# A two-layer decoder trunk: a longer table of small weights, and the first keys normed and rotated before the fifth weight split

## What is computed

```python
def reference(x, ...):
    # layer 0
    x = x + nsa_fox_mixer(rmsnorm(x, a_norm), a_w_in, ...)   # compressed, selected and window attention (8 heads, 2 key groups) + forgetting attention (8 heads)
    x = x + swiglu(rmsnorm(x, f_norm), f_w_gate, f_w_up, f_w_down)      # D_FF = 2816
    # layer 1
    x = x + gla_mixer(rmsnorm(x, c_norm), c_w_in, ...)                  # gated linear attention, 4 heads
    x = x + moe_ffn(rmsnorm(x, m_norm), m_router, m_w_gate, ...)        # best 2 of 8 SwiGLU experts
    return x

# in nsa_fox_mixer: the keys that this change touches
    ksl = partial_rope(rmsnorm(heads(ksl, G), nsa_k_norm), cos, sin)    # selected keys, 2 heads of 64
    kwn = partial_rope(rmsnorm(heads(kwn, G), nsa_k_norm), cos, sin)    # window keys, 2 heads of 64
```

## Time and profile before

| | |
|---|---|
| three runs | 1252.96 us median (1251.99 to 1253.08) |
| the profiled execution | 1252.75 us |
| its span, first to last instruction | 1250.9 us, so 1.85 us lie around it |
| busy: PE, DVE, ACT | 99%, 79%, 65% of the span |
| granted TensorE clock | 0.996 of full, mean |
| HBM read | 354.56 MB, mean 288 GB/s with the writes |

### The profile page before, as it was taken

One profiled execution on the slowest core, in us unless ns is written; L12 is line 12 of the kernel. 1 busy time (PEld: TensorE's weight loads), 2 busy tenths in 40 slices (PEclk: granted clock), 3 DMA queues, 4 the chain that ended last, 5 costly groups with the idle time before them and its releaser, 6 DMA issues.

```text
span 1250.9 us, 16182 instructions
## 1 busy us (share of the span) xinstructions
PE 1233.9 (99%) x6016; PEld 1021.7 (82%) x6021; DVE 982.4 (79%) x966; ACT 817.2 (65%) x891; POOL 36.5 (3%) x42
## 2 busy tenths in 40 slices
PE   8999999999999999999999999999999999999998
PEld 6789888888889886888888888888888888888886
DVE  5878664544567558999889889889889889889896
ACT  7555454343376547777777777777777777777774
POOL 1000000000000001000000000000000000000200
PEclk9899999999999999999999999999999999999999
DMA  9631135544444345999999999999999999999992
GB/s 356 253 135 35 53 150 202 202 179 172 169 184 143 131 152 201 361 392 373 398 365 375 398 365 371 398 372 368 395 355 368 408 381 368 387 369 364 396 420 92
DMA packets 53000, 361.36 MB, mean 289 GB/s; under 512 B 6048, under 2 KB 6560, under 8 KB 10944
## 3 DMA queue, kind: packets, MB, share of 16 engines
q1 hardware_dynamic: 49872, 349.34, 72.4%
q0 software_dynamic: 3056, 11.02, 2.2%
HBM read 354.56 MB, written 5.77 MB: 288 GB/s over the span
## 4 chain that ended last, share of the span: by engine, by line
PE 94%; DVE 2%; DMA 1%; SPq 1%; issue 1%; ACT 0%; DVEq 0%
PE bank L561 28%; PE bank L559 28%; PE bank L560 28%; PE bank L1099 2%; DMA raw<-in_weights 1%; PE bank L770 1%; PE bank L800 1%; PE bank L958 1%; PE bank L782 1%; PE bank L569 1%; PE bank L1064 0%; PE bank L669 0%; PE bank L846 0%; PE bank L716 0%; PE bank L1056 0%
## 5 line engine op out<-in xcount | busy, mean ns | idle before, releaser
L2150 DVE TENSOR_TENSOR low<-raw,whi 128x2048 fp32r<-128x2048 f32 x260 | 595.1, 2291 | 72.0 <-ACT whi L1497 70.8
L1497 ACT CAST whi<-raw 128x2048 fp32r<-128x2048 f32 x260 | 497.3, 1913 | 120.8 <-PE bank L561 119.8
L559 PE MATMUL bank<-whi,hT_hi 128*128 128x512 f32 (+1 forms) x1104 | 431.4, 391 | 1.7 <-DVE low L1646 1.1
L561 PE MATMUL bank<-whi,hT_lo 128*128 128x512 f32 (+1 forms) x1104 | 430.5, 390 | 0.0
L560 PE MATMUL bank<-low,hT_hi 128*128 128x512 f32 (+1 forms) x1104 | 429.8, 389 | 0.0
L559 PEld LDWEIGHTS bank<-whi,hT_hi 128*128 128x128 f32 x1104 | 208.1, 188 | 46.0 <-DVE hT_lo L1581 1.5
L560 PEld LDWEIGHTS bank<-low,hT_hi 128*128 128x128 f32 x1104 | 207.8, 188 | 43.8
L561 PEld LDWEIGHTS bank<-whi,hT_lo 128*128 128x128 f32 x1104 | 207.7, 188 | 43.1
L1563 DVE TENSOR_TENSOR low<-raw,whi 128x2048 fp32r<-128x2048 f32 x67 | 153.0, 2288 | 48.3 <-ACT whi L1190 48.2
L559 PE MATMUL bank<-whi,h_hi 128*128 128x512 f32 x440 | 183.1, 416 | 0.0
L561 PE MATMUL bank<-whi,h_lo 128*128 128x512 f32 x440 | 174.5, 397 | 0.0
(11 more groups left out here) (313 smaller groups left out, 823.6 us busy)
## 6 DMA issues: line engine op xcount, KB each, us to landing
raw<-in_weights SPq DMA_DIRECT2D x327, 1024.0 KB, 5.9
sums<-ybuf POOLq DMA_DIRECT2D x7, 512.0 KB, 6.9
arena<-in_compress SPq DMA_DIRECT2D x1, 1088.0 KB, 15.4
x<-in_x SPq DMA_DIRECT2D x2, 512.0 KB, 5.2
raw<-in_weights SPq DMA_DIRECT2D x4, 256.0 KB, 5.4
raw<-in_weights SPq DMA_DIRECT2D x2, 512.0 KB, 8.1
tokens<-hng POOLq DMA_DIRECT2D x2, 512.0 KB, 3.5
out<-x SPq DMA_DIRECT2D x4, 256.0 KB, 3.0
```

Of the source, the lines that this page charges most:

```text
L559: mm(out_, a_hi, b_hi, start=start, stop=False)
L561: return mm(out_, a_lo, b_hi, start=False, stop=stop)
L1497: nc.scalar.copy(whi[:, u % SPLIT, :, :], raw[:, u % RAW, :, :]).then_inc(S["w_hi"], 1)
L2150: V.tensor_tensor(low[:, u % RAW, :, :], raw[:, u % RAW, :, :], whi[:, u % SPLIT, :, :].bitcast(F32), ALU.subtract).then_inc(S["w_lo"], 1)
```

## The change

Three things are edited:

- The table `sml` is 550 words wide and not 426: the parts from `R_ON` on begin at column 256, so that columns 131 to 255 hold nothing. The first of its two late loads carries 290 columns (145 KB) and not 166 (83 KB). The table's place in SBUF stays, everything declared behind it moves up by 480 bytes: `arena` begins at byte 164480, `h2_hi` at 168576, `h2_lo` at 170624, all multiples of 64. `ybuf` and `mtab` go from a multiple of 64 to 32 over one.
- On ACT the squares of the first keys come behind the two copies of group 0. PE, before group 2 that writes the same banks, waits for the squares.
- On DVE the norm and the rotation of the first keys come in front of `split(5)`.

```diff
-R_QN, R_KN, R_FQ, R_FK, R_ON, R_GB, R_FB, R_EPS = 0, 64, 128, 129, 130, 132, 156, 164
-R_NORM = 166
+R_QN, R_KN, R_FQ, R_FK, R_ON, R_GB, R_FB, R_EPS = 0, 64, 128, 129, 256, 258, 282, 130
+R_NORM = 290
...
             def in_group(cg, hooks=None):
                 if cg >= 2:
                     pe.wait_ge(S["proj"], 2 * (cg - 1))
+                if cg == 2:
+                    pe.wait_ge(S["squares"], 2)
...
                 act.wait_ge(S["units_used"], 2 * (cg + 1))
-                if cg == 0:
-                    head_squares(0, 0, 256)
...
                 if cg == 0:
+                    head_squares(0, 0, 256)
                     head_root(0, 8)
...
             head_sums(4, 0)
-            split(5)
             dve.wait_ge(S["const_in"], 16)
...
             rope(keys, tab, 4, four(rA, 4), four(rB, 4)).then_inc(S["head_done"], 1)
+            split(5)
             dve.wait_ge(S["sw_hi"], 2)
```

## The result

Four runs of the changed kernel gave 1241.48 us median (1240.93 to 1243.23), four of the kernel before 1253.02 (1251.99 to 1253.41). The ratio is 0.9912, 95% interval 0.9894 to 0.9929: faster, by 11.5 us by the medians, 11.0 (8.9 to 13.3) by the ratio. The forecast was 1244.9, so both gains are there and 3.4 us more.

A forecast was written before the change was run, and what follows sets the result against it. PE was taken as the bound, busy 1233.9 of 1250.9 us. From the profiled 1252.75 us, 1.3 for the wait and 6.6 for the place were subtracted, giving 1244.9 us; range 1240.0 to 1251.6.

The forecast's parts named there:

- The squares behind the copies: On ACT at the front, squares and copies change places and PE's added wait has 3.4 us to spare: no gain.
- The wait before the compression: PE's idle wait after group 2 goes, as DVE's norm and rotation start earlier: 1.3 us gained.
- The clock: Half-clock stretch from 45.1 to 51.8 us behind PE's wait: difference put at 0, up to 3.4 us either way.
- The table's load: 124 more columns on SP's queue delay later loads by 0.15 us, hidden behind DVE's chain: no cost.
- The place: Down products: h2 moved onto a multiple of 64 bytes takes hT's shorter step, 0.06 us on 110 blocks: 6.6 us gained.
- rival 3: Down products on h2: the new place against the weight stream is worse, one more 0.0057 us step each: 1259.0 us, chance 0.04.
- The page that spoke against it: Trainium skill on SBUF alignment, read as giving no gain from moving h2; with the TensorE page, a sum of 1251.5 us.

The follow-up runs named there:

- the pad alone: Kernel before with only 32 bytes more padding behind the table, putting arena, hact and h2 on multiples of 64 bytes: 1251.91 us, ratio 0.9998.
- DVE's order undone: Changed kernel with the split of unit 5 put back in front of the norm on DVE, all else kept: 1245.89 us, ratio 0.9945.
- table alone: Kernel before with only the long table and its load, instructions in the old order: 1244.69 us, ratio 0.9948.

## Why the prediction was right, and where its steps failed

*Right in sign and range, 3.4 us too high.* Two terms were sized too small, and one had the wrong rule.

*The squares behind the copies: 0, right.* The timeline of ACT in the changed kernel:

```profile
26.18 1.26 ACT L1290 ACTIVATE arena<-bank,rstd 128x512 f32<-128x512 f32 x2
27.33 0.84 ACT L1244 ACTIVATE hn<-bank,rstd 128x256 f32<-128x256 f32 x2
```

and that of DVE:

```profile
28.52 0.68 DVE L1600 TENSOR_REDUCE arena<-hn 128x8 f32<-128x512 f32 x1
...
29.91 0.20 DVE L1606 RECIPROCAL arena<-arena 128x8 f32<-128x8 f32 x1 [0.50 <-ACT arena L1250]
...
33.13 2.29 DVE L1564 TENSOR_TENSOR low<-raw,whi 128x2048 fp32r<-128x2048 f32 x1
35.34 0.42 DVE L1671 TENSOR_TENSOR sw<-sml,sw 128x64 fp32r<-128x64 f32 x2
```

The squares end at 28.17, and DVE's sums begin at 28.52, behind DVE's own split, as predicted.

*The wait before the compression: -1.3, right.* Norm to rotation take 3.3 us (29.91 to 33.22), the split of unit 5 ends at 35.42, PE wants it at 36.74, and DVE has its last block at 40.8, with PE free for it at about 42.2. All stands some 1.1 to 1.5 us later than forecast: already the first product of group 1, which no edit precedes but the table's load, came 1.1 us later (23.97 us; 22.86 before); the order and the slack (1.3 us, forecast 1.6) are those of the prediction.

*The clock: put at 0, and that was the first step that failed.* "Nothing in the rows says which" was true of the one profile; the choice of the nearest row hid 2 to 3 us. The fall stands in three of the four profiles with DVE's old order (before, the pad alone, DVE's order undone) and in none of the ten with the new one. In executions with the old order and the wait, compression to group 3 took 4.64 us at full clock (table alone, 42.62 to 47.26), and with the fall 6.44 (before, 42.56 to 49.00) and 7.11 (DVE's order undone, 42.77 to 49.88). With the wait the front gives 3.2 to 4.4 us (table alone against the changed kernel, and DVE's order undone against it), not 1.3. A part is paid later: in the profiled execution the attention's own stretch at 1.2 GHz is longer, and the lead falls from 3.4 to 1.8 us. That varies; in the run with everything 64 further (1241.61 us in the profile) only a part of 81.00 to 87.70 is at 1.2 GHz. Why the clock fell behind the wait in three executions and not in the fourth is not shown.

*The table's load: 0, right within what can be told.* With the new order and h2 32 off, the long table gave 1249.39 us and the short one 1249.06; the runs of each spread over 2.8 us.

*The place: -6.6, and -8.0 measured.* The size fell short since I priced a block on h2 at its new place like twelve products on hT behind the same transposes, 4.21 us; it is 4.19, and before 4.27: 0.08 us, not 0.06, on 110 blocks. A part of that is the 2.8 us that go with `arena` and `hact`, which the prediction had counted at nothing because the transposes' own durations are the same; what changes stands behind them.

*The rule behind that term was wrong.* "hT begins on a multiple of 64 bytes, h2 32 bytes past one" was one difference, and the wrong one to pick: on a multiple of 64, 64 bytes away, h2 gained nothing. What fits every run is rival 3's thought, that the step follows from how the stationary tile lies against the stream, with the opposite sign: the new place, aligned with the stream, is the better one. `low` begins at byte 16512, `whi` at 82048, `hT_hi` at 131200, and all stationary tiles with short steps lie a whole number of 512 bytes from both: hT 224 x 512 behind `low` and 96 x 512 behind `whi`, h2 now 169 x 512 behind `whi`. h2 lay at 168 x 512 + 32 before. In the runs, distances that are 32, 64, 128 or 224 bytes off a multiple of 512 cost 4 to 7 ns a product, whichever tile was moved.

A rival that the experiments leave, since ACT and DVE write `whi` and `low`, is that these writes are what collides with PE's reads. The trace of the kernel before speaks against it. In its last block the other engines and the DMA do nothing for 3.2 us, and the steps there are the long ones, 0.233 us (start:end, length, busy PE to POOL, PEclk, DMA share, GB/s):

```profile
1238.00:1241.20 3.20, 3.20 (x15) 2.61 (x14) 0.00 (x0) 0.00 (x0) 0.00 (x0) 1.00 0.00 0
```

Reached by the wrong rule, the forecast got the right place by luck: 480 bytes are right for both rules, and 32 would have been right for mine alone.

*The page that spoke against it.* The prediction read the Trainium skill ("SBUF — State Buffer", Specifications, "Operand start alignment") as if by it nothing moved. That is more than the page says: it calls its rule on starts a matter of legality, not speed, and its own runs timed nothing. For these products the runs here did: 128 bytes, eight of the page's lines of 16, made hT's step 0.2326 instead of 0.2270 us, and the kernel, with h2 moved too, 23.6 us slower.

What stays open: whether 512 or 256 is the period (256 was moved only together with another shift), what collides (the records of the weight loads have the same mean of 188 to 189 ns at either place), why one displaced product in three costs as much as three, the share of `hact` against `arena`, and what decides whether the clock falls behind the wait.

## What to carry to other kernels

Read the step from start to start for each stationary tile apart: 6 ns on 4584 products is 2% of this kernel, and no page of busy shares shows it. When two tiles of one shape differ, compare their addresses not with a round number but with the tile that they work against, and try the place alone before believing a rule: a pad of one line refuted mine. An idle stretch of PE can cost more than its length where the clock falls behind it; price the fall as a second outcome with a chance, not at zero.

## What was not expected of the hardware

- The step of a 128 x 512 float32 product goes with the distance between its stationary and its moving tiles in SBUF: 0.2270 us at a whole number of 512 bytes, 0.231 to 0.2335 at the other distances tried, and again 0.2265 to 0.2272 with all tiles moved by 64 bytes.
- With one of three products displaced (`h2_lo` alone) the three steps sum to 0.700 us, as with all displaced; aligned, 18 steps in 4.09 us, they sum to 0.682.
- One idle stretch of PE of about 1.1 us, before the same 64 small matmuls, was followed by a stretch at 1.2 GHz in one execution and not in another (0.54 and 1.00 in 45.10:51.80).
